# Where the pre-norm weights are applied: in front of the transposes of x on Pool, or behind them on ScalarE and VectorE

## The chip, the cores and the metric

The kernel runs on one core of one Trainium2 chip. The metric is the device time of one execution in microseconds (us), smaller being better. In the profile PE is TensorE (matmuls and transposes), PEld its loading of weights, ACT is ScalarE, DVE is VectorE, POOL is GpSimd and SP is SyncE, which only issues transfers.

## The reference

A model of two layers on x of 256 tokens by 2048 features, all in float32. Around each of the four sub-layers stands an RMS norm on both sides:

```
for layer in range(DEPTH):
    h = rms_norm(x, norm_mix_pre[layer])
    ...
    x = x + rms_norm(m.astype(x.dtype), norm_mix_post[layer])
    h = rms_norm(x, norm_ffn_pre[layer])
    f = swiglu(h, ffn_w_gate[layer], ffn_w_up[layer], ffn_w_down[layer])
    x = x + rms_norm(f.astype(x.dtype), norm_ffn_post[layer])
```

`rms_norm(x, g)` is x / sqrt(mean(x^2) + eps) * g, with g a vector of 2048 weights. The first mixer is a recurrence and an attention side by side, the second an attention with a difference of two maps. What matters here is that h, in each of the four places, is x times the pre-norm weights g, feature by feature, times one number per token. The kernel applies that number (`rstd_x`) when it reads the products, and g before it.

## The kernel before

**Tiles.** Every product is made of slots. A slot is a 512x512 block of a weight matrix (1 MB) against four k tiles of the input, for both halves of the tokens (t = 0 and 1, 128 tokens each). Because float32 is split into a high and a low part, each k tile needs three matmuls, high by high, low weight by high input, high weight by low input: 12 matmuls of 512 columns for one half, 24 for a slot. For a weight, SP loads `raw`, ScalarE writes `w_hi` (function `hi`, L710) and VectorE writes `w_lo` (function `lo`, L1097). A half of a slot is the task `half`, and `half(slot, t, turn)` puts a tile's transposes behind the first three matmuls of the half.

**Boundaries.** Between two sub-layers stands a boundary. There are five: 0 at the start (the chunks of x come from memory), 1 between mixer and FFN of layer 0, 2 between the layers, 3 between mixer and FFN of layer 1, 4 at the end (no input tile is made there). The function `boundary` writes the order of boundaries 1 to 4 out by hand as one list of tasks; every engine walks through the same list and takes its share of each task. s0 to s3 are the last four slots before the boundary (one for each chunk of 512 output features), e, f, g and h the first four slots behind it (one for each chunk of 512 input features), and u is the number of s0. For each chunk c and half t the steps are:

- `add_output`: VectorE adds the product to `yacc` (L1135); `y_square`: ScalarE squares it and sums (L726).
- `rms_y(t)`: VectorE makes the mean (L1113, L1115), Pool the reciprocal root (L1364). It needs the squares of all four chunks of the half.
- `y_gain`: Pool multiplies `yacc` by the post-norm weights (L1372).
- `update(c, t)`: VectorE writes x = x + y * rstd (L1126). Behind it Pool writes x times the pre-norm weights to `tok` (even c) or `stage` (odd c), in `gained` (L1387).
- `turn(c, t)`, a task of kind `T`: PE transposes four blocks of 128x128 from there into one PSUM bank `tp` (L951), ScalarE copies the bank to `h_hi` (L731) and VectorE writes `h_lo`, the bank minus `h_hi` (L1102). I write T00 for c = 0 and t = 0, T10 for c = 1 and t = 0.

The halves behind the boundary come in the order e 0, f 0, e 1, f 1, g 0, g 1, h 0, h 1, and each can start when its tile is ready: T00, T10, T01, T11, T20, T21, T30, T31 (the last half, h 1, needs T31).

The pre-norm weights of a boundary come by a transfer of their own, broadcast to all 128 partitions: 1 MB into `gx` for boundaries 1 to 3 (`gains`), and four pieces of 256 KB at the start, each behind its chunk of x in SP's queue. `gx` holds other things in between, so these transfers wait for Pool's multiplies (`xg_done`).

## Time and profile before

| | us |
|---|---|
| median of 3 runs | 2328.31 (2327.73 to 2328.93) |
| the profiled execution | 2329.11 |
| its span, first to last instruction | 2327.3 |

The span is cut at the instructions; the time of an execution has a little around it. The mean granted clock of TensorE over the span was 0.993, where 1 is 2.4 GHz and 0.5 is 1.2 GHz. A row of a timeline gives the start in us from the span's start, the duration, the engine, the line of the kernel, what it writes and reads, and in square brackets how long the engine was idle before it and who released it. The duration of a matmul includes what overlaps with the next one, so a matmul's share of PE's time is read from start to start.

### The profile page before, as it was taken

The page shows a single profiled execution, that of the slowest core. Times are in us where ns is not written, and L with a number is a line of the kernel's source. Part 1 is how long each engine was busy: PE and PEld are TensorE (multiplying, and loading weights), DVE is VectorE, ACT ScalarE, POOL GpSimd, SP SyncE. Part 2 cuts the span into 40 slices and gives each one's busy share as a digit, 9 for nine tenths or more (in the row PEclk, how much of TensorE's full clock was granted, in tenths as well). Part 3 has the DMA queues.
Part 4 walks back from the last instruction along what each step waited for, and adds up shares of the span by engine and source line. Part 5 has one row for each costly group of instructions (what it writes and reads, how often), then busy time and mean ns, then how long its engine had stood idle before and what let it go on. Part 6 is the DMA issues. An engine that isn't in the chain of part 4 may idle for free.

```text
span 2327.3 us, 27257 instructions
## 1 busy us (share of the span) xinstructions
PE 2273.3 (98%) x10273; PEld 1858.9 (80%) x10273; DVE 1313.6 (56%) x1308; ACT 1033.7 (44%) x1131; POOL 253.3 (11%) x243
## 2 busy tenths in 40 slices
PE   8989999899999999999999999999999999999997
PEld 6877778688888888888777777887888888888886
DVE  4567466654555555554655555676545555555555
ACT  5676444533333333343455555545434333333432
POOL 2463001400000000000340111014000000000002
PEclk9999999999999999999999999999999999999999
DMA  8545344555555555555454444555556555555552
GB/s 277 168 139 168 124 165 153 205 185 188 192 195 184 197 183 197 183 196 191 152 182 153 155 162 144 199 167 187 189 183 196 190 188 193 185 197 182 196 187 102
DMA packets 212263, 417.87 MB, mean 180 GB/s; under 512 B 12040, under 2 KB 12640, under 8 KB 211296
## 3 DMA queue, kind: packets, MB, share of 16 engines
q1 hardware_dynamic: 212192, 416.92, 54.3%
q8 instruction: 45, 0.74, 0.1%
q14 instruction: 26, 0.21, 0.0%
HBM read 414.79 MB, written 2.10 MB: 179 GB/s over the span
## 4 chain that ended last, share of the span: by engine, by line
issue 71%; PE 20%; POOL 4%; DVE 3%; DMA 1%; ACT 1%; SPq 0%; POOLq 0%; DVEq 0%; ACTq 0%
PE acc L937 16%; POOL yacc L1372 1%; PE tp L951 1%; DVE xs L1126 1%; DVE w_lo L1097 1%; PE sc L1018 1%; DMA gq<-in_norm_ffn_post 1%; POOL stage L1387 0%; PE sc L1023 0%; POOL small L1364 0%; PE sc L996 0%; POOL gq L1436 0%; PE pv L996 0%; POOL rot L1406 0%; PE pv L1051 0%
## 5 line engine op out<-in xcount | busy, mean ns | idle before, releaser
L1097 DVE TENSOR_TENSOR w_lo<-raw,w_hi 128x2048 fp32r<-128x2048 f32 x383 | 883.2, 2306 | 512.4 <-PE acc L937 495.3
L710 ACT ACTIVATE w_hi<-raw 128x2048 fp32r<-128x2048 f32 x383 | 734.2, 1917 | 759.5 <-PE acc L937 734.6
L937 PE MATMUL acc<-w_hi,h_hi 128*128 128x512 f32 x2240 | 888.6, 397 | 16.7 <-DVE h_lo L1102 16.7
L937 PE MATMUL acc<-w_hi,h_lo 128*128 128x512 f32 x2240 | 874.7, 390 | 0.0
L937 PE MATMUL acc<-w_lo,h_hi 128*128 128x512 f32 x2240 | 874.4, 390 | 0.0
L937 PEld LDWEIGHTS acc<-w_hi,h_hi 128*128 128x128 f32 x2240 | 422.5, 189 | 111.3 <-DVE h_lo L1102 23.4
L937 PEld LDWEIGHTS acc<-w_hi,h_lo 128*128 128x128 f32 x2240 | 421.7, 188 | 89.1
L937 PEld LDWEIGHTS acc<-w_lo,h_hi 128*128 128x128 f32 x2240 | 422.5, 189 | 84.9 <-issue 0.7
L937 PE MATMUL acc<-w_hi,y_hi 128*128 128x512 f32 x832 | 325.8, 392 | 1.9 <-DVE y_lo L1102 1.9
L937 PE MATMUL acc<-w_hi,y_lo 128*128 128x512 f32 x832 | 323.9, 389 | 0.0
L937 PE MATMUL acc<-w_lo,y_hi 128*128 128x512 f32 x832 | 323.9, 389 | 0.0
L1135 DVE TENSOR_TENSOR yacc<-acc,yacc 128x512 f32<-128x512 f32 x208 | 141.7, 687 | 163.6 <-PE acc L937 163.6
L1372 POOL TENSOR_TENSOR yacc<-yacc,gq 128x512 f32<-128x512 f32 x32 | 48.5, 1522 | 1554.9 <-ACT junk L726 1554.9
L937 PEld LDWEIGHTS acc<-w_hi,y_hi 128*128 128x128 f32 x832 | 156.2, 188 | 37.3 <-issue 2.9
L937 PEld LDWEIGHTS acc<-w_hi,y_lo 128*128 128x128 f32 x832 | 156.2, 188 | 32.6
L937 PEld LDWEIGHTS acc<-w_lo,y_hi 128*128 128x128 f32 x832 | 156.2, 188 | 32.1 <-issue 0.2
L807 ACT ACTIVATE probT<-tp 128x256 f32<-128x256 f32 (+1 forms) x48 | 21.9, 457 | 123.6 <-PE pv L1051 64.4
L900 ACT ACTIVATE y_hi<-tp 128x512 fp32r<-128x512 f32 x44 | 24.2, 596 | 87.8 <-PE tp L951 87.8
L1324 DVE SCALAR_TENSOR_TENSOR tok<-acc,small,stage 128x512 f32<-128x512 f32 x44 | 33.0, 751 | 52.8 <-PE acc L937 52.8
L894 ACT ACTIVATE stage<-acc,small 128x512 f32<-128x512 f32 x44 | 30.2, 690 | 56.6 <-PE acc L937 56.5
L1406 POOL TENSOR_TENSOR rot<-stage,ropes 128x128 f32<-128x128 f32 x24 | 21.7, 902 | 284.3 <-ACT stage L748 283.0
L951 PE MATMUL tp<-ident,tok 128*128 128x128 f32 x288 | 40.1, 278 | 11.7 <-POOL tok L1387 9.4
(142 smaller groups left out, 1058.8 us busy)
## 6 DMA issues: line engine op xcount, KB each, us to landing
raw<-in_ffn_w_gate SPq DMA_DIRECT2D x88, 1024.0 KB, 5.1
raw<-in_ffn_w_up SPq DMA_DIRECT2D x88, 1024.0 KB, 5.1
raw<-in_ffn_w_down SPq DMA_DIRECT2D x88, 1024.0 KB, 5.0
raw<-in_od_w_in SPq DMA_DIRECT2D x48, 1024.0 KB, 5.1
...
```

Of the source, the lines that this page charges most:

```text
L710: act.activation(w_hi[u % HI][:, :, :], raw[u % RAW][:, :, :], ACT.Copy).then_inc(hi_done, 1)
L807: act.activation(flat_pt[:, 0:cols], flat_tp[:, 0:cols], ACT.Copy).then_inc(tp_free[task.e % 2], 1)
L894: act.activation(stage[:, t, :], acc[n % 2][t][:, :], ACT.Silu, scale=rstd_x[:, t:t + 1]).then_inc(acc_free[n % 2][t], 1)
L900: act.activation(y_hi[:, 0:KT, t * P:(t + 1) * P], tp[t][:, :, :], ACT.Copy).then_inc(t_hi, 1)
L937: mm = pe.matmul(acc[n % 2][t][:, :], operand(lhs, a, k, t), w[:, k, :], start=first and k == 0 and j == 0, stop=last and k == KT - 1 and ...
L951: ins = pe.transpose(dst, src, ident[:, :])
L1018: pe.matmul(sc[:, :, :].rearrange("p m t -> p (m t)"), q[:, kt, t * P:(t + 1) * P], keys[task.g % 2][:, kt, :, :].rearrange("p m t -> p (m ...
L1097: dve.tensor_tensor(w_lo[u % LO][:, :, :], raw[u % RAW][:, :, :], w_hi[u % HI][:, :, :].bitcast(F32), ALU.subtract).then_inc(lo_done, 1)
L1126: dve.scalar_tensor_tensor(r, yacc[:, task.t, cols], rstd_y[:, task.t:task.t + 1], r, ALU.mult, ALU.add).then_inc(upd_done, 1)
L1135: dve.tensor_tensor(y, a, y, ALU.add).then_inc(acc_free[n % 2][t], 1)
L1324: dve.scalar_tensor_tensor(tok[:, t, :], acc[n_up % 2][t][:, :], rstd_x[:, t:t + 1], stage[:, t, :], ALU.mult, ALU.mult).then_inc(acc_free ...
L1372: pool.tensor_tensor(y, y, post_gain[:, cols], ALU.mult).then_inc(yg_done, 1)
```

## The change

Pool's multiply in front of the transposes is gone. PE transposes x itself. ScalarE applies the pre-norm weights while it writes the high part: behind the transpose a feature is a partition, so the weights of a 128x128 block are one column, given to ScalarE as a scale. VectorE does the same while it writes the low part. A column fits one block only, so both work in four pieces of 128x128 in place of one of 128x512. The four blocks lie in two PSUM banks, the first two in `tp`, the last two in `sc` or `pv`; VectorE's pieces wait for ScalarE's in pairs (`x_hi`). The weights of all four places come once, at the start, as one transposed array `pre` of 32 KB, prepared with the arrays of constants; the broadcasts to `gx` and the waits on `xg_done` are gone. The hand-written order of a boundary changes in one place: T00 now stands inside the last half before the boundary (s3, t = 1), `add_output` of that half stands behind T00, and `hi(u + 6)` moves behind the last square. `y_gain` waits for the square of its own tile, in place of all the squares listed so far.

```diff
@@ -304,8 +304,8 @@
             tasks += [update(c, 1), update(c + 1, 1), Task("store", c=c, t=1)]
         return tasks
     e, f, g, h = after
-    tasks += [hi(u + 6), update(1, 0), y_square(s2, 1)] + half(s3, 1) + add_output(s3, 1)
-    tasks += [turn(0, 0), y_square(s3, 1), rms_y(1), y_gain(1, 1), lo(u + 5), update(0, 1)]
+    tasks += [update(1, 0), y_square(s2, 1)] + half(s3, 1, turn(0, 0)) + add_output(s3, 1)
+    tasks += [y_square(s3, 1), hi(u + 6), rms_y(1), y_gain(1, 1), lo(u + 5), update(0, 1)]
     tasks += half(e, 0, turn(1, 0)) + [hi(u + 7), update(1, 1)]
     tasks += half(f, 0, turn(0, 1)) + [y_gain(2, 1), square(0, 0), update(2, 0)]
     tasks += half(e, 1, turn(1, 1)) + [y_gain(3, 0), square(1, 0), square(0, 1), lo(u + 6), update(2, 1)]
...
@@ -322,15 +322,17 @@
         if task.kind == "T":
             task.e = plan.e
             plan.e += 1
-            buffer = "tok" if task.src == "tok" or (task.src == "x" and task.g % 2 == 0) else "stage"
-            plan.read[buffer, task.t] = task.e
+            if task.src != "x":
+                plan.read["tok" if task.src == "tok" else "stage", task.t] = task.e
             key = {"x": ("x", task.b), "tok": ("y", task.layer)}.get(task.src, (task.src, task.layer))
             plan.ready[(*key, task.g, task.t)] = task.e
-            if task.src in ("x", "tok"):
+            if task.src == "tok":
                 task.m = plan.m
                 plan.m += 1
             if task.src == "x":
-                task.gained = plan.gained[task.b, task.g, task.t]
+                task.m = plan.xm
+                task.update = plan.update.get((task.b, task.g, task.t))
+                plan.xm += KT
         elif task.kind == "pt":
             task.e = plan.e
             plan.e += 1
...
@@ -343,8 +345,10 @@
             task.sq, task.update = plan.squares, plan.update.get((task.b, task.c, task.t))
             task.stat = plan.stat.get(("rms_x", task.b - 1, 0))
             plan.squares += 1
+            if task.kind == "y_square":
+                plan.squared[task.b, task.slot.cb, task.t] = plan.squares
         elif task.kind == "y_gain":
-            task.sq, task.gained = plan.squares, plan.y_gains
+            task.sq = plan.squared[task.b, task.c, task.t]
             plan.y_gained[task.b, task.c, task.t] = plan.y_gains
             plan.y_gains += 1
         if task.kind in ("evac", "silu"):
...
@@ -580,8 +584,10 @@
                 return [b[:, kt:kt + KT, t * P:(t + 1) * P] for b in (h_hi, h_lo)]
             return [b[:, KT * task.g:KT * (task.g + 1), t * P:(t + 1) * P] for b in (y_hi, y_lo)]
 
-        def x_buffer(c):
-            return tok if c % 2 == 0 else stage
+        def input_tile(e, k):
+
+            bank = tp[e % 2] if k < KT // 2 else (sc, pv)[e % 2][:, :, :].rearrange("p a (b c) -> p (a b) c", b=2)
+            return bank[:, k, :]
 
 
         @block.sync
...
@@ -601,7 +607,6 @@
 
                 cols = slice(c * KC, (c + 1) * KC)
                 sp.dma_start(xs[:, :, cols], x_rows[:, :, cols]).then_inc(x_in[c], 16)
-                sp.dma_start(pre_gain[:, cols], norm_mix_pre[0, cols].partition_broadcast(P)).then_inc(x_in[c], 16)
 
             def load_parameters():
...
@@ -631,14 +636,8 @@
                     sp.wait_ge(rg_out, RG_OUT * AT)
                 else:
                     sp.wait_ge(yg_done, 8 * (b - 1))
-                    sp.wait_ge(xg_done, 8 * b)
-                if b == 3:
-                    sp.wait_ge(s_done, 16 + 3 * HEADS_OF_GROUP)
                 post = norm_mix_post[b // 2] if b % 2 else norm_ffn_post[b // 2 - 1]
-                sp.dma_start(post_gain, post.partition_broadcast(P)).then_inc(gain_in[0], 16)
-                if b < 4:
-                    pre = norm_ffn_pre[b // 2] if b % 2 else norm_mix_pre[b // 2]
-                    sp.dma_start(pre_gain, pre.partition_broadcast(P)).then_inc(gain_in[1], 16)
+                sp.dma_start(post_gain, post.partition_broadcast(P)).then_inc(gain_in, 16)
 
             def load_slot(slot):
                 block = NF - 1 if slot.w == "down" else slot.kg
...
@@ -747,8 +747,21 @@
                     func = ACT.Gelu_apprx_tanh if task.what == "gate" else ACT.Copy
                     act.activation(dst, acc[slot][t][:, :], func, scale=rstd_x[:, t:t + 1]).then_inc(acc_free[slot][t], 1)
 
+            def input_hi(task):
+
+                act.wait_ge(pre_in, 16)
+                act.wait_ge(tp_done, task.e + 1)
+                dst = region_of(task)[0]
+                for k in range(KT):
+                    kt = KT * task.g + k
+                    act.activation(dst[:, k, :], input_tile(task.e, k), ACT.Copy,
+                                   scale=pre[:, task.b, kt:kt + 1]).then_inc(x_hi, 1)
+
             def transposed(task):
-                if task.src in ("x", "tok"):
+                if task.src == "x":
+                    input_hi(task)
+                    return
+                if task.src == "tok":
                     operand_hi(task)
                     return
                 act.wait_ge(tp_done, task.e + 1)
...
@@ -964,8 +975,11 @@
                     product(slot.u, slot.n, slot.lhs, slot.first, slot.last, task.t, task.k)
                 elif task.kind == "T":
                     if task.src == "x":
-                        pe.wait_ge(xg_done, task.gained + 1)
-                        src = x_buffer(task.g)
+                        if task.b:
+                            pe.wait_ge(upd_done, task.update + 1)
+                        else:
+                            pe.wait_ge(x_in[task.g], 16)
+                        src = xs[:, :, task.g * KC:(task.g + 1) * KC]
                     elif task.src == "tok":
                         if task.layer == 0:
                             pe.wait_ge(o_done, task.head + 1)
...
@@ -978,7 +992,10 @@
                             pe.wait_ge(rope_done, task.evac.rope + task.t + 1)
                         else:
                             wait_acc(pe, task.evac.n, task.t)
-                    transposes(task.e, quarter(task.e, src, task.t))
+                    if task.src == "x":
+                        transposes(task.e, [(input_tile(task.e, k), src[:, task.t, k * P:(k + 1) * P]) for k in range(KT)])
+                    else:
+                        transposes(task.e, quarter(task.e, src, task.t))
                 elif task.kind == "par" and task.i == 0:
 
                     pe.wait_ge(par_in, 16 * 12)
...
@@ -1101,6 +1118,16 @@
                 dve.wait_ge(t_hi, m + 1 + NT * it)
                 dve.tensor_tensor(lo_ap, tp[e % 2][:, :, :], hi_ap.bitcast(F32), ALU.subtract).then_inc(tp_free[e % 2], 1)
 
+            def input_lo(task):
+
+                hi_ap, lo_ap = region_of(task)
+                for k in range(KT):
+                    kt = KT * task.g + k
+                    dve.wait_ge(x_hi, task.m + k // 2 * 2 + 2)
+                    ins = dve.scalar_tensor_tensor(lo_ap[:, k, :], input_tile(task.e, k), pre[:, task.b, kt:kt + 1],
+                                                   hi_ap[:, k, :].bitcast(F32), ALU.mult, ALU.subtract)
+                ins.then_inc(tp_free[task.e % 2], 1)
+
             def mean(task):
 
                 if task.kind == "rms_x":
...
@@ -1366,25 +1395,10 @@
             def y_gain(task):
 
                 pool.wait_ge(sq_done, task.sq)
-                pool.wait_ge(gain_in[0], 16 * task.b)
+                pool.wait_ge(gain_in, 16 * task.b)
                 cols = slice(task.c * KC, (task.c + 1) * KC)
                 y = yacc[:, task.t, cols]
                 pool.tensor_tensor(y, y, post_gain[:, cols], ALU.mult).then_inc(yg_done, 1)
-
-            def gained(task):
-
-                if task.b == 4:
-                    return
-                if task.b == 0:
-                    pool.wait_ge(x_in[task.c], 32)
-                else:
-                    pool.wait_ge(upd_done, task.update + 1)
-                    pool.wait_ge(gain_in[1], 16 * task.b)
-                last = (task.stage_free if task.c % 2 else task.tok_free)[task.t]
-                if last is not None:
-                    pool.wait_ge(tp_done, last + 1)
-                cols = slice(task.c * KC, (task.c + 1) * KC)
-                pool.tensor_tensor(x_buffer(task.c)[:, task.t, :], xs[:, task.t, cols], pre_gain[:, cols], ALU.mult).then_inc(xg_done, 1)
 
             def rotate(task):
...
@@ -1439,15 +1453,12 @@
 
             def zero_keys():
 
-                pool.wait_ge(xg_done, 8 * 3)
                 pool.wait_ge(s_done, 16)
                 for buf in keys:
                     pool.memset(buf[:, :, :, :], 0.0).then_inc(keys_zero, 1)
 
             def task_of(task):
-                if task.kind == "update":
-                    gained(task)
-                elif task.kind == "y_gain":
+                if task.kind == "y_gain":
                     y_gain(task)
                 elif task.kind in ("rms_x", "rms_y"):
                     rsqrt(task)
...
@@ -1460,15 +1471,11 @@
                 elif task.kind == "heads":
                     pool.wait_ge(sub_var_done, task.g + 1)
                     pool.tensor_tensor(sub_r, sub_var, minus_half, ALU.pow).then_inc(sub_rstd, 1)
-                if task.kind == "update" and task.b == 0 and task.c == NC - 1 and task.t == NT - 1:
-
-
-                    for i in range(2):
-                        pool.memset(rg_w[i], 0.0).then_inc(zero_done, 1)
-                    pool.wait_ge(xg_done, 8)
-                    pool.memset(xrT[:, :, 0:CONV // 2], 0.0).then_inc(zero_done, 1)
-                    pool.memset(xrT[:, :, CONV // 2 + T:XP], 0.0).then_inc(zero_done, 1)
-
+
+            for i in range(2):
+                pool.memset(rg_w[i], 0.0).then_inc(zero_done, 1)
+            pool.memset(xrT[:, :, 0:CONV // 2], 0.0).then_inc(zero_done, 1)
+            pool.memset(xrT[:, :, CONV // 2 + T:XP], 0.0).then_inc(zero_done, 1)
             for part in plan.parts:
                 for task in part.tasks or ():
                     task_of(task)
...
@@ -1504,6 +1511,8 @@
     arrays["log_count"] = log_counts()
     arrays["rope"] = rope_tables()
     arrays["identity"] = np.eye(P, dtype=np.float32)
+    pre = np.stack([arrays["norm_mix_pre"], arrays["norm_ffn_pre"]], axis=1)
+    arrays["pre_T"] = np.ascontiguousarray(pre.reshape(4, D // P, P).transpose(2, 0, 1))
     args = [nc.dram_tensor(f"in_{n}", a.shape, mybir.dt.from_np(a.dtype), kind="ExternalInput").ap()
             for n, a in arrays.items()]
     args.append(nc.dram_tensor("out_0", arrays["x"].shape, F32, kind="ExternalOutput").ap())
```

The places in the order of instructions, first on PE, at the end of slot s3 in boundary 1 (acc11 is the sum of s3 for t = 1, acc00 that of e for t = 0). Before:

```order
L937 MATMUL acc11<-w_hi3,h_hi 128x512
L937 MATMUL acc11<-w_lo1,h_hi 128x512
L937 MATMUL acc11<-w_hi3,h_lo 128x512
L951 MATMUL tp0<-ident,tok 128x128 x4
L937 MATMUL acc00<-w_hi0,h_hi 128x512
L937 MATMUL acc00<-w_lo2,h_hi 128x512
L937 MATMUL acc00<-w_hi0,h_lo 128x512
```

Now:

```order
L948 MATMUL acc01<-w_hi2,h_lo 128x512
L948 MATMUL acc11<-w_hi3,h_hi 128x512
L948 MATMUL acc11<-w_lo1,h_hi 128x512
L948 MATMUL acc11<-w_hi3,h_lo 128x512
L962 MATMUL tp0<-ident,xs 128x128 x2
L962 MATMUL sc<-ident,xs 128x128 x2
L948 MATMUL acc11<-w_hi3,h_hi 128x512
L948 MATMUL acc11<-w_lo1,h_hi 128x512
L948 MATMUL acc11<-w_hi3,h_lo 128x512
L948 MATMUL acc11<-w_hi3,h_hi 128x512
L948 MATMUL acc11<-w_lo1,h_hi 128x512
```

T00 has moved ahead of nine matmuls of the last half; its four transposes read x, and write two banks.

On VectorE, at the same place, from the first update of the boundary on. Before:

```order
L1126 SCALAR_TENSOR_TENSOR xs<-yacc,small,xs 128x512
L1135 TENSOR_TENSOR yacc<-acc,yacc 128x512
L1126 SCALAR_TENSOR_TENSOR xs<-yacc,small,xs 128x512
L1135 TENSOR_TENSOR yacc<-acc,yacc 128x512
L1102 TENSOR_TENSOR h_lo<-tp,h_hi 128x4x128
L1113 TENSOR_REDUCE small<-small 128x1
L1115 TENSOR_SCALAR small<-small 128x1
L1097 TENSOR_TENSOR w_lo<-raw,w_hi 128x2048
L1126 SCALAR_TENSOR_TENSOR xs<-yacc,small,xs 128x512
L1102 TENSOR_TENSOR h_lo<-tp,h_hi 128x4x128
L1126 SCALAR_TENSOR_TENSOR xs<-yacc,small,xs 128x512
```

Now (the lines have moved: L1153 is the update, L1162 `add_output`, L1127 the pieces of a tile, L1114 a weight's low part):

```order
L1153 SCALAR_TENSOR_TENSOR xs<-yacc,small,xs 128x512
L1162 TENSOR_TENSOR yacc<-acc,yacc 128x512
L1153 SCALAR_TENSOR_TENSOR xs<-yacc,small,xs 128x512
L1127 SCALAR_TENSOR_TENSOR h_lo<-tp,pre,h_hi 128x128 x2
L1127 SCALAR_TENSOR_TENSOR h_lo<-sc,pre,h_hi 128x128 x2
L1162 TENSOR_TENSOR yacc<-acc,yacc 128x512
L1140 TENSOR_REDUCE small<-small 128x1
L1142 TENSOR_SCALAR small<-small 128x1
L1114 TENSOR_TENSOR w_lo<-raw,w_hi 128x2048
L1153 SCALAR_TENSOR_TENSOR xs<-yacc,small,xs 128x512
L1127 SCALAR_TENSOR_TENSOR h_lo<-tp,pre,h_hi 128x128 x2
```

The add in front of the mean (L1113 before, L1140 now) has gone from ahead of T00 to behind it.

On ScalarE, from the last squares of the boundary's first half of tokens on. Before:

```order
L726 ACTIVATE junk,small<-yacc 128x512 x2
L710 ACTIVATE w_hi<-raw 128x2048
L726 ACTIVATE junk,small<-yacc 128x512
L731 ACTIVATE h_hi<-tp 128x4x128
L726 ACTIVATE junk,small<-yacc 128x512
L731 ACTIVATE h_hi<-tp 128x4x128
L710 ACTIVATE w_hi<-raw 128x2048
L731 ACTIVATE h_hi<-tp 128x4x128
```

Now:

```order
L710 ACTIVATE w_hi<-raw 128x2048
L726 ACTIVATE junk,small<-yacc 128x512 x3
L757 ACTIVATE h_hi<-tp,pre 128x128 x2
L757 ACTIVATE h_hi<-sc,pre 128x128 x2
L726 ACTIVATE junk,small<-yacc 128x512
L710 ACTIVATE w_hi<-raw 128x2048
L757 ACTIVATE h_hi<-tp,pre 128x128 x2
L757 ACTIVATE h_hi<-pv,pre 128x128 x2
```

The weight's high part (L710) that stood ahead of the last square but one stands behind the last one, and a tile is four instructions.

## Rows read from the trace of the kernel before

**Rows 1.** The page: each engine's busy time, its share of the span, its instructions

```profile
PE 2273.3 (98%) x10273; PEld 1858.9 (80%) x10273; DVE 1313.6 (56%) x1308; ACT 1033.7 (44%) x1131; POOL 253.3 (11%) x243
```

**Rows 2.** List of waits: us in total, times, longest

```profile
PE acc L937 <- DVE h_lo L1102: 16.7, 16, 2.0
```

**Rows 3.** Timeline of PE, boundary 1: start us, us, what, idle before it

```profile
406.45 0.39 PE L937 MATMUL acc<-w_hi,h_hi 128*128 128x512 f32 x1
...
408.94 0.39 PE L937 MATMUL acc<-w_hi,h_lo 128*128 128x512 f32 x1
409.62 0.66 PE L951 MATMUL tp<-ident,tok 128*128 128x128 f32 x4 [0.29 <-POOL tok L1387]
411.69 0.50 PE L937 MATMUL acc<-w_hi,h_hi 128*128 128x512 f32 x1 [1.41 <-DVE h_lo L1102]
...
414.79 0.40 PE L937 MATMUL acc<-w_hi,h_lo 128*128 128x512 f32 x1
416.98 0.50 PE L937 MATMUL acc<-w_hi,h_hi 128*128 128x512 f32 x1 [1.79 <-DVE h_lo L1102]
...
427.50 0.50 PE L937 MATMUL acc<-w_hi,h_hi 128*128 128x512 f32 x1 [0.65 <-DVE h_lo L1102]
...
432.72 0.50 PE L937 MATMUL acc<-w_hi,h_hi 128*128 128x512 f32 x1 [1.72 <-DVE h_lo L1102]
...
436.61 0.50 PE L937 MATMUL acc<-w_hi,h_hi 128*128 128x512 f32 x1 [0.40 <-DVE h_lo L1102]
```

**Rows 4.** Timeline of DVE, boundary 1

```profile
407.44 0.75 DVE L1126 SCALAR_TENSOR_TENSOR xs<-yacc,small,xs 128x512 f32<-128x512 f32 x1 [0.69 <-POOL small L1364]
...
410.04 0.68 DVE L1135 TENSOR_TENSOR yacc<-acc,yacc 128x512 f32<-128x512 f32 x1
410.94 0.69 DVE L1102 TENSOR_TENSOR h_lo<-tp,h_hi 128x512 fp32r<-128x512 f32 x1 [0.23 <-ACT h_hi L731]
...
411.83 2.29 DVE L1097 TENSOR_TENSOR w_lo<-raw,w_hi 128x2048 fp32r<-128x2048 f32 x1
414.57 1.76 DVE L1126 SCALAR_TENSOR_TENSOR xs<-yacc,small,xs 128x512 f32<-128x512 f32 x1 [0.44 <-POOL small L1364]
416.25 0.68 DVE L1102 TENSOR_TENSOR h_lo<-tp,h_hi 128x512 fp32r<-128x512 f32 x1
...
428.69 3.38 DVE L1097 TENSOR_TENSOR w_lo<-raw,w_hi 128x2048 fp32r<-128x2048 f32 x1
```

**Rows 5.** Timeline of ACT, boundary 1

```profile
408.88 0.63 ACT L726 ACTIVATE junk<-yacc 128x512 bf16<-128x512 f32 x1
...
410.31 0.60 ACT L731 ACTIVATE h_hi<-tp 128x512 fp32r<-128x512 f32 x1 [0.70 <-PE tp L951]
```

**Rows 6.** Timeline of POOL, boundary 1

```profile
429.88 3.33 POOL L1387 TENSOR_TENSOR stage<-xs,gx 128x512 f32<-128x512 f32 x1
```

**Rows 7.** Timeline of DVE, attention of layer 1, pieces of 128x128

```profile
1302.32 2.19 DVE L1198 SCALAR_TENSOR_TENSOR tok<-tok,small,sub_gain 128x128 f32<-128x128 f32 x8 [1.76 <-POOL small L1462]
```

**Rows 8.** Timeline of ACT, attention of layer 1, sizes without a scale column

```profile
1249.61 0.39 ACT L807 ACTIVATE probT<-tp 128x256 f32<-128x256 f32 x1 [3.52 <-PE pv L1051]
1249.89 0.30 ACT L817 ACTIVATE probT<-tok 128x128 f32<-128x128 f32 x1
```

**Rows 9.** Timeline of ACT, recurrence, with a column as operand

```profile
159.23 0.47 ACT L842 ACTIVATE yacc<-sc,par 128x256 f32<-128x256 f32 x1 [0.17 <-PE pv L996]
```

**Rows 10.** Timeline of PE, boundary 2

```profile
1158.55 0.50 PE L937 MATMUL acc<-w_hi,h_hi 128*128 128x512 f32 x1 [0.23 <-DVE h_lo L1102]
```

**Rows 11.** Timeline of PE, recurrence of layer 0

```profile
155.41 2.08 PE L996 MATMUL sc<-gq 128*128 128x256 f32 x4 [5.51 <-POOL gq L1436]
```

**Rows 12.** Busy time by window; behind POOL stands the granted clock (PEclk)

```profile
153.50:160.30 6.80, 4.89 (x12) 3.89 (x13) 3.23 (x4) 3.74 (x7) 6.33 (x7) 0.50 0.00 0
1153.60:1157.00 3.40, 3.40 (x12) 2.73 (x11) 2.96 (x2) 1.51 (x2) 3.40 (x2) 0.50 0.10 7
```

**Rows 13.** Timeline of all engines, start of the kernel

```profile
11.64 0.80 PE L937 MATMUL acc<-w_hi,h_hi 128*128 128x512 f32 x1 [2.02 <-DVE h_lo L1102]
```

25 lines of the change are left out of this document (13 added, 12 removed).

## The prediction

> **What bounds the kernel now.** I read the page first. TensorE is busy for 98% of the span, so what can be won or lost is its idle time; DVE, at 56%, is far from full on average [rows 1]. The list of waits then says where TensorE idles for this part of the program: `PE acc L937 <- DVE h_lo L1102`, 16 waits, 16.7 us in all [rows 2]. That is a matmul waiting for the low part of an input tile, which is what the change rebuilds. Third I read the timeline of PE across the boundary at 405 to 441 us (mixer to FFN of layer 0) [rows 3]. Matmuls start every 0.227 us (12 from 406.45 to 408.94), except for five pauses, each released by `h_lo`: before the half of slot e at 411.69 (1.41 us), of f at 416.98 (1.79), of g at 427.50 (0.65) and 432.72 (1.72), of h at 436.61 (0.40). Together 6.0 us. I call them e0, f0, g0, g1, h0. Boundaries 2 and 3 have the same five, with a shorter one ahead of f0 (0.23 us in boundary 2, [rows 10]); why is said below.
>
> Last I read the timeline of DVE there [rows 4], to see why `h_lo` is late. DVE is busy back to back: an update of x, a weight's low part (L1097), a tile's low part (L1102). Two things stretch it. The update that runs beside nothing takes 0.75 us, the one at 414.57 beside Pool's multiply takes 1.76; and L1097 takes 2.29 us alone (411.83) but 3.38 beside Pool (428.69; Pool's own multiply runs from 429.88 for 3.33 us) [rows 4, 6]. So the boundary is a chain on DVE, not on Pool: Pool's multiply ahead of T00 costs PE only a pause of 0.29 us at 409.62 [rows 3].
>
> **Pool's part.** 8 multiplies fall away at each boundary. I take an update beside which they ran at 0.75 us and L1097 at 2.29, except where one of the four multiplies by the post-norm weight (L1372) still runs: these now follow each other directly behind the second rsqrt, so the update at 414.57 keeps its 1.76 us.
>
> **A tile's part.** Today ScalarE starts the high part at 410.31 and the low part ends at 410.94 + 0.69 = 411.63: 1.32 us for a tile, 0.68 of it DVE's [rows 4, 5]. After it there are four pieces of 128x128 on each engine. DVE has a row of that operation and size: eight in 2.19 us, 0.35 each and 0.26 from start to start [rows 7], so four take 0.35 + 3 x 0.26 = 1.13 us, 0.45 more than the whole tile. ScalarE has no such row. 128x128 without a scale column took 0.30 us; 128x256 took 0.39 without and 0.47 with a column, so the column costs 0.08; starts lie 0.11 closer than durations [rows 8, 9]. That gives 0.38 us, 0.27 from start to start. DVE's first piece may begin when two are done, at 0.27 + 0.38 = 0.65; its third when four are, at 1.19. With 0.03 us to be released the low part ends at 1.22 + 0.26 + 0.35 = 1.83 us behind ScalarE's start, 0.5 later than today.
>
> The Trainium skill, "ScalarE: Activation LUTs", section "What ACT_TABLE_LOAD costs", prices an ACTIVATE with one pointer operand at about 280 ns + 0.833 ns per element, with neighbours overlapping by 93 ns. By that a piece would be an estimated 0.39 us, 0.29 from start to start, and a tile would end 0.1 us later than in my sum; the nearest rows here agree to 0.01 us in the duration. By the page the total would be about 0.5 us higher.
>
> **The moved tile.** T00 now stands behind the first three matmuls of the last half before the boundary, on PE. Those end at 406.45 + 0.68 = 407.13, but the first update ends at 408.19 (407.44 + 0.75), so T00 starts at 408.27 and PE pauses 1.14 us inside that half. A half without a tile takes 2.72 us (406.45 to 408.94, + 0.23), one with a tile 3.33 (411.69 to 414.79, + 0.23), so a tile takes 0.61. The half ends at 408.27 + 0.61 + 9 x 0.227 = 410.92, in place of 409.17 [rows 3, 4]. ScalarE takes T00 only behind the square that it starts at 408.88 [rows 5], so at 409.51; the low part ends at 411.34 and e0 starts at 411.40: 0.29 us won.
>
> What is late next is the second half of tokens. `add_output` of that half, before at 410.04 and in front of T00's low part, now stands behind it on DVE: 411.26 to 411.94. The square, the mean and then L1097 follow it; today L1097 starts 1.11 us behind the end of the add (411.83 against 410.72) [rows 4], so now 413.05, 1.22 later. Behind it on DVE are queued the update at 414.57, now 415.79, and the low part of tile T10, which started at 416.25, now 417.47, and takes 1.13: 418.60. f0 waits for it: 418.66 against 416.98, **1.68 us lost**. `hi(u+6)` on ScalarE, moved behind the last square, ends by 415, and its low part is wanted at 425: nothing.
>
> From there, in the same way:
> - from f0 on come two halves without a pause today; a tile's way within a half (0.7 us of matmuls, 0.1, 0.69 from transpose to ScalarE, 1.83) is 3.3 us, just the length of a half. No loss, and no slack either.
> - g0 stands behind a weight (2.29), an update (0.75) and T20 (1.13), starts overlapping by 0.08, from 425.03 on: 429.14 against 427.50, 1.64 late.
> - g1: behind an update, a weight and a tile, 3.93 us in place of today's 5.22 (427.50 to 432.72): 433.07, 0.35 late. Here the relief from Pool pays, 1.3 us.
> - h0: 3.93 in place of 3.89: 0.39 late. h1 is bound by PE.
>
> So each boundary ends 0.4 us later at full clock, 1.2 us for three.
>
> **The clock.** PE's pause ahead of f0 grows from 1.96 (414.79 + 0.23 to 416.98) to 3.93 us (414.73 to 418.66). In boundary 2 the granted clock stands at 0.50, 1.2 GHz, from 1153.60 to 1157.00, behind the pause ahead of e0 [rows 12]; its cost is swallowed there, f0 still waits 0.23 us for `h_lo` at 1158.55 [rows 10]. Boundary 1 has the same pause at full clock. A longer pause, 5.51 us up to 155.41 [rows 11], has the clock at 0.50 from 153.50 to 160.30, so for 4.9 us of the work behind it [rows 12]. For 3.9 us I take the lower clock as likely, and as reaching 1.0 to 3.4 us into f0: at half rate this costs 0.5 to 1.7 us, and nothing swallows it, because f0 and the two halves behind it are bound by PE. I take 1.2: 3.6 us for three.
>
> **The start and the queues.** The first matmul, at 11.64, waits for `h_lo`, which is made behind the first weights [rows 13]. Of 1344 KB queued up to those weights (512 for x, 256 for `gx`, 64 for the identity, 512 of weights) 256 leave and 32 come, a sixth of less than 8 us; the first tile ends up to 0.45 us later on DVE. I take 0.3 us won, between 0 and 0.9. Three transfers of 1 MB (`gx`) also leave SP's queue, and their waits with them; none of the five pauses was ended by a transfer, so nothing. The looser wait of `y_gain` changes nothing where Pool stands behind the second rsqrt anyway. The last boundary has no tiles: nothing.
>
> **Sum**: 1.2 + 3.6 - 0.3 = 4.5 us. The profiled execution took 2329.11 us (span 2327.3), so 2333.6 in its terms; it stands 0.80 above the median of the runs, 2328.31, so 2332.8.
>
> **Bounds.** A piece on DVE lies between 0.17 us (a quarter of today's 0.68) and 0.75 (a whole update, alone); I stay with the row of its own shape. On ScalarE between 0.15 (a quarter of 0.60) and 0.47. With the lower ends a tile costs as today: four tiles on DVE's chain, 0.45 each, 1.8 us a boundary, and the clock may hold: 2323. With ScalarE's upper end and 1.7 us for the clock: about 1.5 us more a boundary, 2337; a DVE piece of 0.40 adds another 2.
>
> **The rivals.**
> - *Forecast*, 35%: 2332.8.
> - *The clock holds ahead of f0*, 25%: 1.2 - 0.3 alone, 2329.2. For it speaks boundary 1, which kept 2.4 GHz through a pause like that of the other two.
> - *Small pieces are dear, or the lower clock costs its full 1.7 us*, 28%: 2337 to 2339. For it speaks that tiles have no slack inside a half, so each 0.1 us more is paid at about six tiles of a boundary.
> - *Relief from Pool decides, faster*, 12%: 2322.3. Place: g0, g1 and h0, where weights fall from 3.38 to 2.29 us on DVE. If a tile stays at about 0.68 us there and the clock holds, f0 is 1.22 late, DVE is through with T20 before PE needs it, so g0 at 428.05, g1 at 431.38 and h0 at 434.71 are bound by PE alone, the last 1.9 us ahead of today: 5.7 for three, 0.3 at the start. It decides below about 0.75 us for a tile on DVE. Against it is the row of eight pieces at 0.26 us from start to start.
>
> Anything within 0.2% (4.7 us) can't be told from no change. Above 2333.0 lie the case of dear pieces and about half of the forecast's own spread: slower 0.45, same 0.43, faster 0.12. Range 2325 to 2339; it leaves out most of the faster case.
>
> **What would show it.** In the changed kernel's profile: four pieces near 0.38 us on ScalarE and 0.35 on DVE per tile; T00 on PE right behind an update, with a pause of about 1.1 us inside a half; f0 10.5 us behind the end of the boundary's first update (408.19 to 418.66) where it was 8.8; a granted clock of 0.5 just behind f0's pause; weights at 2.29 us throughout g and h. I am wrong if f0 isn't later than today relative to that update, which would mean that DVE's order there isn't what holds the second half, or if a tile on DVE costs well off 1.13 us.

## The result and the profile after

The changed kernel takes 2337.59 us (median of 6 runs, 2334.85 to 2338.42) against 2328.1 (6 runs, 2327.73 to 2328.93): 0.4% slower, ratio 1.0037 (95% interval 1.0027 to 1.0047). The profiled execution took 2336.99 us, 7.9 more than that of before. The medians differ by 9.5: the profiled execution of before stands 1.0 above its median and the changed kernel's 0.6 below, so 1.6 us of the loss are in neither of the two traces. The page and the list of waits (us in total, times, longest), as [rows 1, 2]:

```profile
span 2335.2 us, 27407 instructions
PE 2277.3 (98%) x10273; PEld 1860.3 (80%) x10273; DVE 1311.3 (56%) x1404; ACT 1049.5 (45%) x1227; POOL 198.6 (9%) x211
...
PE acc L948 <- DVE h_lo L1127: 21.5, 18, 3.8
```

Pool lost 55 us of work and DVE a little, and neither shows in the time. PE waits 4.8 us more for the low parts of the input tiles. The timeline of PE at boundary 1 (start, duration, what, idle before it), as [rows 3]:

```profile
408.01 0.39 PE L948 MATMUL acc<-w_hi,h_lo 128*128 128x512 f32 x1
409.34 0.44 PE L962 MATMUL tp<-ident,xs 128*128 128x128 f32 x2 [0.95 <-DVE xs L1153]
...
412.43 0.50 PE L948 MATMUL acc<-w_hi,h_hi 128*128 128x512 f32 x1 [0.38 <-DVE h_lo L1127]
...
415.52 0.40 PE L948 MATMUL acc<-w_hi,h_lo 128*128 128x512 f32 x1
419.67 0.50 PE L948 MATMUL acc<-w_hi,h_hi 128*128 128x512 f32 x1 [3.75 <-DVE h_lo L1127]
...
421.17 0.63 PE L948 MATMUL acc<-w_lo,h_hi 128*128 128x512 f32 x1
421.60 0.63 PE L948 MATMUL acc<-w_hi,h_lo 128*128 128x512 f32 x1
```

Three things are to be seen. T00 makes PE pause inside the half (409.34 - 408.01 - 0.227 = 1.1 us). The pause ahead of f0 has grown to 419.67 - 415.52 - 0.23 = 3.92 us. And 1.5 us into f0 the matmuls start every 0.43 us instead of every 0.227. What f0 waits for stands on DVE, as [rows 4]:

```profile
408.54 0.75 DVE L1153 SCALAR_TENSOR_TENSOR xs<-yacc,small,xs 128x512 f32<-128x512 f32 x1 [0.68 <-POOL small L1393]
...
411.25 0.61 DVE L1127 SCALAR_TENSOR_TENSOR h_lo<-tp,pre,h_hi 128x128 fp32r<-128x128 f32 x2 [0.70 <-ACT h_hi L757]
411.78 0.60 DVE L1127 SCALAR_TENSOR_TENSOR h_lo<-sc,pre,h_hi 128x128 fp32r<-128x128 f32 x2
412.29 0.68 DVE L1162 TENSOR_TENSOR yacc<-acc,yacc 128x512 f32<-128x512 f32 x1
413.83 0.16 DVE L1140 TENSOR_REDUCE small<-small 128x1 f32<-128x4 f32 x1 [0.85 <-ACT junk L726]
414.02 0.15 DVE L1142 TENSOR_SCALAR small<-small 128x1 f32<-128x1 f32 x1
414.10 2.29 DVE L1114 TENSOR_TENSOR w_lo<-raw,w_hi 128x2048 fp32r<-128x2048 f32 x1
416.83 1.75 DVE L1153 SCALAR_TENSOR_TENSOR xs<-yacc,small,xs 128x512 f32<-128x512 f32 x1 [0.44 <-POOL small L1393]
418.50 0.59 DVE L1127 SCALAR_TENSOR_TENSOR h_lo<-tp,pre,h_hi 128x128 fp32r<-128x128 f32 x2
419.02 0.59 DVE L1127 SCALAR_TENSOR_TENSOR h_lo<-pv,pre,h_hi 128x128 fp32r<-128x128 f32 x2
```

The `add_output` at 412.29 stands behind T00's low part, and everything behind it is queued: mean, weight, update, T10. It starts 3.00 us behind the end of the boundary's first update (409.29), where it stood 1.85 behind it before (410.04 against 408.19): 1.15 us later. T10's four pieces, from 418.50 to 419.61, then take 0.4 us more than the one operation did. Together that is the 1.6 us that f0 comes later. ScalarE's pieces of T00 and Pool's two operations beside this stretch, as [rows 5, 6]:

```profile
410.61 0.61 ACT L757 ACTIVATE h_hi<-tp,pre 128x128 fp32r<-128x128 f32 x2
411.11 0.62 ACT L757 ACTIVATE h_hi<-sc,pre 128x128 fp32r<-128x128 f32 x2
```

```profile
414.25 2.54 POOL L1393 TENSOR_TENSOR small<-small 128x1 f32<-128x1 f32 x1 [5.75 <-DVE small L1142]
416.77 4.64 POOL L1401 TENSOR_TENSOR yacc<-yacc,gq 128x512 f32<-128x512 f32 x3
```

Busy time by window, the granted clock (PEclk) behind POOL, in the stretches behind f0's pause of boundaries 1, 2 and 3, as [rows 12]:

```profile
421.10:424.50 3.40, 3.40 (x9) 2.64 (x8) 1.79 (x5) 1.75 (x6) 1.56 (x2) 0.50 0.00 0
...
1161.80:1168.60 6.80, 5.43 (x15) 4.36 (x16) 3.76 (x11) 1.87 (x7) 4.35 (x3) 0.50 0.37 139
...
1588.40:1591.80 3.40, 3.04 (x9) 2.56 (x10) 0.96 (x3) 0.44 (x2) 3.33 (x3) 0.51 0.48 187
```

At each boundary of this execution TensorE runs at 1.2 GHz behind that pause.

In the table below all starts are of PE, in us from the end of the boundary's first update (boundary 1; 408.19 before, 409.29 after), with the kernels of the experiments, which the next section describes. A column is a half (e1 is slot e, t = 1; f1 is left out), a row is a kernel (e1 is an experiment). The last column is the time from the last matmul of e0's half to f0, less the 0.23 us of that matmul; in w1 it is filled with transposes.

| | e0 | f0 | e1 | g0 | g1 | h0 | h1 | pause ahead of f0 |
|---|---|---|---|---|---|---|---|---|
| before | 3.50 | 8.80 | 12.10 | 19.32 | 24.53 | 28.42 | 31.75 | 1.96 |
| after | 3.15 | 10.38 | 15.26 | 22.38 | 26.28 | 30.18 | 33.52 | 3.92 |
| w1 | 3.15 | 10.39 | 13.74 | 20.98 | 24.88 | 28.78 | 32.12 | 3.94 |
| e1 | 3.52 | 9.32 | 12.67 | 19.91 | 23.81 | 27.71 | 31.07 | 0.95 |
| e3 | 3.08 | 8.37 | 11.70 | 18.10 | 21.41 | 24.95 | 28.26 | 1.98 |
| b1 | 5.55 | 12.70 | 18.67 | 25.09 | 30.07 | 33.96 | 37.29 | 3.95 |
| c1 | 3.14 | 8.19 | 12.07 | 19.31 | 23.20 | 27.10 | 30.44 | 1.74 |
| v1 | 3.61 | 8.51 | 11.74 | 18.43 | 21.87 | 25.21 | 28.55 | 0 |
| v4 | 3.61 | 7.54 | 10.88 | 17.57 | 21.02 | 24.35 | 27.69 | 0.61 |

### The profile page after: what moved, and what is told of

The parts are those of the page before. It is cut to its first block, busy times and chain, and to the rows that moved or that the text cites. A ratio compares the mean times of both kernels' runs of the same rounds, so it can differ in the third digit from the quotient of the medians.

```text
span 2335.2 us, 27407 instructions
## 1 busy us (share of the span) xinstructions
PE 2277.3 (98%) x10273; PEld 1860.3 (80%) x10273; DVE 1311.3 (56%) x1404; ACT 1049.5 (45%) x1227; POOL 198.6 (9%) x211
## 4 chain that ended last, share of the span: by engine, by line
PE 58%; issue 33%; DVE 4%; POOL 2%; ACT 2%; DMA 1%; SPq 0%; DVEq 0%; ACTq 0%; POOLq 0%
PE acc L948 53%; PE tp L962 2%; DVE w_lo L1114 2%; PE sc L1035 1%; PE sc L1040 1%; DVE h_lo L1127 1%; DVE xs L1153 1%; PE pv L1063 1%; PE pv L1068 0%; POOL small L1393 0%; PE sc L1013 0%; POOL gq L1450 0%; PE pv L1013 0%; ACT w_hi L710 0%; POOL rot L1420 0%
## 5 line engine op out<-in xcount | busy, mean ns | idle before, releaser
L1114 DVE TENSOR_TENSOR w_lo<-raw,w_hi 128x2048 fp32r<-128x2048 f32 x383 | 876.5, 2289 | 508.7 <-PE acc L948 494.1
L710 ACT ACTIVATE w_hi<-raw 128x2048 fp32r<-128x2048 f32 x383 | 734.3, 1917 | 752.3 <-PE acc L948 737.6
L1162 DVE TENSOR_TENSOR yacc<-acc,yacc 128x512 f32<-128x512 f32 x208 | 141.6, 687 | 163.7 <-PE acc L948 163.7
L905 ACT ACTIVATE stage<-acc,small 128x512 f32<-128x512 f32 x44 | 30.2, 690 | 56.6 <-PE acc L948 56.4
L806 ACT ACTIVATE prob<-sc,small 128x256 f32<-128x256 f32 x64 | 29.8, 471 | 26.1 <-DVE small L1180 26.1
```

What stands on the lines that cost most here:

```text
L710: act.activation(w_hi[u % HI][:, :, :], raw[u % RAW][:, :, :], ACT.Copy).then_inc(hi_done, 1)
L806: ins = act.activation(prob[:, m, :], sc[:, m, :], ACT.Exp, scale=SCALE, bias=nmx[:, m:m + 1], accum_out=den[n % 2][:, m:m + 1])
L905: act.activation(stage[:, t, :], acc[n % 2][t][:, :], ACT.Silu, scale=rstd_x[:, t:t + 1]).then_inc(acc_free[n % 2][t], 1)
L1114: dve.tensor_tensor(w_lo[u % LO][:, :, :], raw[u % RAW][:, :, :], w_hi[u % HI][:, :, :].bitcast(F32), ALU.subtract).then_inc(lo_done, 1)
L1162: dve.tensor_tensor(y, a, y, ALU.add).then_inc(acc_free[n % 2][t], 1)
```

## The experiments

The change has two halves: the new order, and the weights in pieces in place of Pool's multiply. Four kernels take them apart. Times are medians; kernel before, beside them, 2328.47.

**e1: the old order in the changed kernel.**

```diff
-    tasks += [update(1, 0), y_square(s2, 1)] + half(s3, 1, turn(0, 0)) + add_output(s3, 1)
-    tasks += [y_square(s3, 1), hi(u + 6), rms_y(1), y_gain(1, 1), lo(u + 5), update(0, 1)]
+    tasks += [hi(u + 6), update(1, 0), y_square(s2, 1)] + half(s3, 1) + add_output(s3, 1)
+    tasks += [turn(0, 0), y_square(s3, 1), rms_y(1), y_gain(1, 1), lo(u + 5), update(0, 1)]
```

> The changed kernel with the order of the boundary as it was: T00 behind the last half, the add of that half and hi(u+6) in front of it. Theory A (the moved tile holds up the second half of tokens on DVE, and the longer pause ahead of f0 lowers the clock): f0 comes 9.4 us behind the end of the boundary's first update (changed kernel 10.4, kernel before 8.8), the pause ahead of it falls from 4 to about 2.5 us, and the time is 1.0 us a boundary less at full clock plus what the clock gives back: 2329 to 2335, most likely 2332. Theory B (the dear pieces are the cause, the order costs nothing): 2337, with f0 at 10.4 us.

Measured 2328.56 us, ratio 1.0002 (0.9993 to 1.0011): no different from before, and better than I expected. PE's pauses at boundary 1 ahead of f0, g0 and g1:

```profile
417.61 0.50 PE L948 MATMUL acc<-w_hi,h_hi 128*128 128x512 f32 x1 [0.76 <-DVE h_lo L1127]
428.20 0.50 PE L948 MATMUL acc<-w_hi,h_hi 128*128 128x512 f32 x1 [0.43 <-DVE h_lo L1127]
432.10 0.50 PE L948 MATMUL acc<-w_hi,h_hi 128*128 128x512 f32 x1 [0.41 <-DVE h_lo L1127]
```

All of the loss is the order's, 9.0 us. With it away, f0 is 0.5 us late by T00's and T10's pieces, and the relief from Pool ahead of g1 more than pays that back: each of the three boundaries ends 0.5 to 0.6 us earlier than before. The pieces at the start of the kernel take that away again (see below).

**e2 and e3: the pre-norm weights left out** (x is transposed into one bank and split as it is, one operation per tile and engine). They don't compute the model; they price the pieces. e2 has the new order, e3 the old.

```diff
...
-                for k in range(KT):
...
-                    act.activation(dst[:, k, :], input_tile(task.e, k), ACT.Copy,
-                                   scale=pre[:, task.b, kt:kt + 1]).then_inc(x_hi, 1)
+                act.activation(dst, tp[task.e % 2][:, :, :], ACT.Copy).then_inc(x_hi, KT)
...
+                dve.tensor_tensor(lo_ap, tp[task.e % 2][:, :, :], hi_ap.bitcast(F32), ALU.subtract).then_inc(tp_free[task.e % 2], 1)
```

> The changed kernel in its new order, but each input tile is one copy and one subtraction of 128x512 again, from one bank, so the pre-norm weights are left out of the computation. Theory A: the pieces cost 0.45 us a tile on DVE; without them the start gains about 1.5 us, f0 is 9.5 us behind the first update and still behind a long pause, g and h are bound by PE: 2325 to 2330. If the order were the only cause, 2336.

> As the run with whole tiles, but with the order of the boundary as it was (the pre-norm weights are left out). Theory A: f0 about 8.5 us behind the first update, no pause long enough to lower the clock for work that isn't hidden, Pool's relief of 1.3 us a boundary or more is won in full: 2320 to 2324. If Pool's multiply had cost DVE nothing, it would be no faster than 2327.

e2 took 2326.92 us (0.9994, 0.9985 to 1.0003), with f0 at 9.8. In its boundary 1 PE's pause was nearly as long as the changed kernel's, and yet the clock held behind it; in boundaries 2 and 3, with pauses of the same length, it fell to 0.5. Boundary 1:

```profile
416.92 0.50 PE L944 MATMUL acc<-w_hi,h_hi 128*128 128x512 f32 x1 [3.58 <-DVE h_lo L1121]
...
416.90:420.00 3.10, 3.08 (x15) 2.57 (x16) 1.97 (x3) 1.21 (x3) 3.10 (x3) 1.00 0.57 218
```

e3 took 2316.94 us (0.995, 0.9937 to 0.9964). e3 was faster than expected: from f0 to g1 PE has no pause left, as my rival of a relief from Pool had it, and no boundary shows the lower clock. Its only two pauses of over 0.3 us at boundary 1:

```profile
411.09 0.50 PE L944 MATMUL acc<-w_hi,h_hi 128*128 128x512 f32 x1 [1.49 <-DVE h_lo L1121]
416.38 0.50 PE L944 MATMUL acc<-w_hi,h_hi 128*128 128x512 f32 x1 [1.83 <-DVE h_lo L1121]
```

So the pieces cost 11.6 us in the old order (2328.56 - 2316.94) and 10.7 in the new (2337.59 - 2326.92), and the order costs 10.0 us with whole tiles too. Apart from the transfers of the weights and `y_gain`'s looser wait, e3 is the kernel before without Pool's multiply, so that multiply costs some 11.5 us (2328.47 - 2316.94): what the change takes away at Pool and what it adds in pieces are equal within the noise, and the order is what is left.

**b1: the new order in the kernel before**, the reverse of e1's edit.

> The kernel before, Pool's multiply included, with only the order of the boundary changed as in the change. Theory A: the last half ends 3.1 us later (412.3 for 409.2), so its add, square and mean and with them f0 come about 2.3 us later, and the pause ahead of f0 grows to 3.7 us and lowers the clock: about 4 us a boundary, 2340. Theory B, the order is innocent: 2328.

Measured 2343.75 us, 1.0058 (1.0045 to 1.0072). f0 is 3.9 us later than before in boundaries 1 and 2 and 2.3 in boundary 3; I had 2.3 for all. e0 is 2.0 us later as well, in 1 and 2, and 0.5 in 3. The granted clock in boundary 1 is 0.5 for 3.4 us from 409.3, behind a pause of 2.3 us inside the last half (T00 waits for Pool), and again for 6.8 us from 419.6; in boundary 3 it held inside the last half. The order alone costs 15.3 us where Pool multiplies ahead of the transposes, so it isn't a gain that the pieces hide.

**w1: PE kept busy in f0's pause.** 32 transposes of the identity, into a bank that nothing reads, behind e0. DVE's chain is untouched. Kernel before, beside w1 and v1 to v3: 2328.35.

```diff
+WARM = 32
...
-    tasks += half(e, 0, turn(1, 0)) + [hi(u + 7), update(1, 1)]
+    tasks += half(e, 0, turn(1, 0)) + [Task("warm"), hi(u + 7), update(1, 1)]
...
+                elif task.kind == "warm":
+                    for k in range(WARM):
+                        pe.transpose(sc[:, 0, 0:P], ident[:, :], ident[:, :])
```

> The changed kernel with 32 extra transposes of the identity (about 3.5 us at the full clock) in PE's pause of 3.9 us ahead of f0, at the three boundaries; they feed nothing. If the lower clock behind that pause costs what the profiles say (1.6, 2.5 and 1.4 us), f0 stays 10.4 us behind the first update, the granted clock stays at 1.0 behind it, and 4 to 5.5 us come back: 2332 to 2334. Rival: the clock falls for other reasons, or the extra transposes delay f0: 2337 or above.

Measured 2332.15 us, 1.0016 (1.0007 to 1.0025), as expected. Windows of w1 at boundary 1, of which the first covers the pause:

```profile
412.00:420.00 8.00, 7.72 (x52) 6.70 (x53) 6.45 (x10) 5.36 (x8) 6.26 (x4) 1.00 0.36 119
420.00:424.00 4.00, 4.00 (x23) 3.17 (x21) 1.79 (x5) 1.76 (x6) 2.18 (x2) 1.00 0.07 28
```

f0 starts at the same place, e1 follows it by 3.35 us instead of 4.88, and the clock stays at 2.4 GHz. What is left per boundary is 0.5 us in each of the three. So the lower clock cost 5.4 us of the 9.5 (2337.59 - 2332.15).

**c1: one update behind T10 instead of ahead of it**, nothing else. Kernel before, beside c1 and v4: 2328.26.

```diff
-    tasks += [y_square(s3, 1), hi(u + 6), rms_y(1), y_gain(1, 1), lo(u + 5), update(0, 1)]
-    tasks += half(e, 0, turn(1, 0)) + [hi(u + 7), update(1, 1)]
+    tasks += [y_square(s3, 1), hi(u + 6), rms_y(1), y_gain(1, 1), lo(u + 5)]
+    tasks += half(e, 0, turn(1, 0)) + [hi(u + 7), update(0, 1), update(1, 1)]
```

> The changed kernel with one task moved in each of boundaries 1 to 3: update(0, 1) stands behind the half of slot e (and so behind tile T10 on VectorE) in place of ahead of it. The chain on VectorE that f0 waits for in the changed kernel is add, weight (2.29 us), mean, update (1.75 us beside Pool), four pieces of T10 (1.13). Theory (that chain, one item at a time, sets f0): f0 falls by the 1.7 us of the update, from 10.38 to about 8.7 us behind the end of the boundary's first update, PE's pause ahead of it from 3.9 to about 2.2 us; T01 has the length of a half to wait for the update, so e1 keeps its place behind f0. At least 3 x 1.7 = 5 us less only if nothing later takes it back: in the changed kernel g0, g1, h0 and h1 are bound by the same chain from T11 on, so that part of it comes back as waits ahead of g0. With the clock: a pause of 2.2 us may or may not bring the half rate. Most likely 2331, between 2328 and 2335. Rival (f0 waits for T10's transposes or for ScalarE): f0 stays at 10.4 and the time at 2337.5.

Measured 2328.05 us, 0.9998 (0.9989 to 1.0007): 9.5 us below the changed kernel, at the lower end of what I gave. DVE at boundary 1:

```profile
415.74 2.29 DVE L1114 TENSOR_TENSOR w_lo<-raw,w_hi 128x2048 fp32r<-128x2048 f32 x1
417.94 0.60 DVE L1127 SCALAR_TENSOR_TENSOR h_lo<-tp,pre,h_hi 128x128 fp32r<-128x128 f32 x2
418.46 0.60 DVE L1127 SCALAR_TENSOR_TENSOR h_lo<-pv,pre,h_hi 128x128 fp32r<-128x128 f32 x2
418.98 2.93 DVE L1153 SCALAR_TENSOR_TENSOR xs<-yacc,small,xs 128x512 f32<-128x512 f32 x2
```

T10 now starts where the weight ends. It wins not only the update (1.75 us) but also DVE's wait for Pool's reciprocal root ahead of it (0.44), so f0 is 2.19 us earlier and its pause, 1.7 us, kept the full clock in all three boundaries. The chain of f0 is shown by this: one item taken out of it moved f0 by that item and the wait ahead of it. The rival, that ScalarE or the transposes hold f0, falls, and with it the thought that `hi(u + 6)`, which now stands ahead of T10 on ScalarE, holds f0. Against w1, where the clock held too, c1 is 4.1 us shorter: so much of the 9.5 us is the chain itself, and 5.4 are the clock.

**v1: the updates and Pool's multiplies in an order of their own.** `pool_wait` makes Pool wait for an update before its next multiply, so that the two don't run beside each other.

```diff
-    tasks += [update(1, 0), y_square(s2, 1)] + half(s3, 1, turn(0, 0)) + add_output(s3, 1)
-    tasks += [y_square(s3, 1), hi(u + 6), rms_y(1), y_gain(1, 1), lo(u + 5), update(0, 1)]
-    tasks += half(e, 0, turn(1, 0)) + [hi(u + 7), update(1, 1)]
-    tasks += half(f, 0, turn(0, 1)) + [y_gain(2, 1), square(0, 0), update(2, 0)]
+    tasks += [pool_wait(0, 0), y_gain(1, 1), y_gain(3, 0), hi(u + 6), update(1, 0), y_square(s2, 1)]
+    tasks += half(s3, 1) + add_output(s3, 1)
+    tasks += [y_gain(2, 1), turn(0, 0), y_square(s3, 1), rms_y(1), lo(u + 5)]
+    tasks += half(e, 0, turn(1, 0)) + [hi(u + 7), update(0, 1), update(1, 1)]
+    tasks += half(f, 0, turn(0, 1)) + [pool_wait(1, 1), y_gain(3, 1), square(0, 0), update(2, 0), update(2, 1), update(3, 0)]
...
```

> The changed kernel with a new order of the boundary, everything computed: T00 behind the last half again, the update (0,1) behind tile T10, three updates ahead of tile T11, weights' low parts behind the tile that is wanted next, Pool's four multiplies drawn forward. If f0 waits for the chain of rsqrt, update and tile on DVE and not for DVE's whole work, f0 comes 7.0 us behind the first update without a pause, h1 27 us (31.1 with the old order), 4 us less a boundary: 2316. Rival: the boundary is bound by the sum of DVE's work, whatever its order: 2326 to 2328.

Measured 2320.92 us, 0.9968 (0.9956 to 0.998), faster than both kernels, but 5 us short of what I expected. PE's only pause of over 0.2 us at boundary 1, the window behind it, and what runs on DVE and Pool there:

```profile
413.08 0.50 PE L952 MATMUL acc<-w_hi,h_hi 128*128 128x512 f32 x1 [2.02 <-DVE h_lo L1131]
...
414.20:417.60 3.40, 3.40 (x11) 2.73 (x10) 3.40 (x7) 2.88 (x5) 2.12 (x1) 0.50 0.13 17
...
413.22 2.69 DVE L1118 TENSOR_TENSOR w_lo<-raw,w_hi 128x2048 fp32r<-128x2048 f32 x1
...
409.56 4.21 POOL L1405 TENSOR_TENSOR yacc<-yacc,gq 128x512 f32<-128x512 f32 x3 [0.86 <-DVE xs L1157]
```

The multiplies drawn forward stretch the weight at 413.22 to 2.69 us (2.29 alone), and e0's pause brings 1.2 GHz in boundaries 1 and 3: f0 is at 8.51 there and at 7.52 in boundary 2, where the clock held. I had 7.0 for all three; the rest of what is missing was not taken apart.

**v2: v1 with a later low part and later squares at the start**, to take away two of PE's waits there.

> As the run before, and at the start of the kernel the squares of x come later on ScalarE and the fourth weight's low part behind tile T30 on DVE. The start had won 1.5 us at the second half and lost 1.9 in two pauses of 0.9 us ahead of the third and fourth slot; if these come from DVE's queue they go: 1.5 us below the run before, 2314.5. Rival: 2316, no change.

Measured 2320.67 us, 0.9968 (0.9956 to 0.998), the same as v1: the rival was right, the pauses only moved to another slot.

**v3: v1's order in the kernel before**, Pool's multiply kept.

> The kernel before, with Pool's multiply and whole tiles, in the same new order of the boundary. It tells what the change is worth once the order is right. If Pool's multiplies beside DVE still stretch the weights' low parts from 2.3 to 3.3 us and put Pool's 1.3 us between an update and its tile, 2318 to 2322, above the changed kernel in that order. Rival: tiles of one piece are worth more than Pool's relief: below 2316.

Measured 2328.5 us, 1.0001 (0.9992 to 1.001): far off what I expected. Pool's timeline, and the transposes that wait for it:

```profile
409.98 3.31 POOL L1391 TENSOR_TENSOR stage<-xs,gx 128x512 f32<-128x512 f32 x1
...
413.35 1.11 PE L955 MATMUL tp<-ident,stage 128*128 128x128 f32 x4 [3.16 <-POOL stage L1391]
```

The multiply for T10 runs beside DVE's weight for 3.31 us, PE waits for it inside e0's half, and f0 comes at 11.8, where v1 has 8.5. Behind that wait the granted clock is 0.5 for 6.8 us in all three boundaries:

```profile
410.00:416.80 6.80, 3.64 (x11) 2.90 (x11) 3.85 (x4) 2.31 (x2) 5.27 (x5) 0.51 0.44 154
```

Here the change of the weights itself is worth something: 7.6 us, 2328.5 against 2320.92. How much of that is the clock was not separated.

**v4: v1 with 16 transposes of the identity in e0's pause**, against 2328.26 before.

```diff
-    tasks += [y_gain(2, 1), turn(0, 0), y_square(s3, 1), rms_y(1), lo(u + 5)]
+    tasks += [y_gain(2, 1), turn(0, 0), y_square(s3, 1), rms_y(1), lo(u + 5), Task("warm")]
```

> The version with moved updates, and 16 transposes of the identity into a bank that nothing reads, on PE in the pause ahead of e0 of boundaries 1 to 3. It computes everything. Theory (the half rate that boundaries 1 and 3 showed behind e0's pause of 2 us costs 1 us each, because f0 has no pause left that swallows it): no granted clock of 0.5 in the boundaries, e0 as before or up to 0.1 us later, about 2 us less: 2319, between 2318 and 2321. Rival (the half rate behind e0 is swallowed by f0's wait): 2321 or slightly above, as without the transposes.

Measured 2318.6 us, 0.996 (0.9946 to 0.9974), the fastest that computes everything: 9.7 us below before, 19.0 below the changed kernel. Windows of v4 at boundary 1:

```profile
409.00:413.00 4.00, 3.72 (x27) 3.13 (x27) 3.97 (x10) 2.48 (x8) 4.00 (x4) 1.00 0.02 6
413.00:417.00 4.00, 3.55 (x19) 2.64 (x18) 4.00 (x7) 2.95 (x5) 2.37 (x1) 1.00 0.17 31
```

No boundary shows the lower clock; f0 is at 7.54 in all three, 0.97 earlier than v1's 8.51, in the two boundaries where v1 lost it.

## Why the prediction was right, and where its sizes were off

The time forecast was 2332.8 and came out at 2337.6: slower, as I gave the largest chance (0.45, with 0.43 for no change), 4.8 us above the sum and inside the range. The mechanism was right and its size was not: the loss is 9.5 us by the medians, twice the 4.5 of the sum, and 7.9 in the profiled executions. That the time still fell inside the range is in part luck: its upper end, 2339, stood for dearer single pieces, which didn't come. By its steps:

- **The moved tile: right.** PE's pause for T00 was to be 1.14 us, it is 1.10. e0 was to start 3.21 us behind the update's end, it starts at 3.15. The add was to start 3.07 behind it; it starts at 412.29 - 409.29 = 3.00.
- **f0: right.** 10.47 forecast, 10.38 measured, pause 3.93 against 3.92. c1 shows the mechanism.
- **A tile's part: right.** ScalarE 0.36 us a piece and 0.25 from start to start (0.38 and 0.27 forecast); DVE 0.35 and 0.26 as in the row I took; T00 from ScalarE's start to the low part's end 412.38 - 410.61 = 1.77 us (1.83). The Trainium skill, "ScalarE: Activation LUTs", section "What ACT_TABLE_LOAD costs", made that an estimated 0.39 and 0.29; the trace lies below it, and the rows of this kernel were the better price.
- **Relief from Pool, g0 to h1: right in the net.** g1 and h0 follow at 3.90 us (3.93 forecast), weights beside them take 2.28. At full clock a boundary ends 0.5 us later (w1), 0.4 forecast. But that is a difference of two sizes that were both too small: by the starts of h1 in the table, Pool's relief alone is 3.5 us a boundary (31.75 before, 28.26 in e3), where my rival had 1.9, and the pieces alone cost 2.8 (31.07 in e1), where my bounds had 1.8. That they cancel was luck.
- **The clock: right in kind, too small.** The term was 3.6 us for three; w1 against the changed kernel gives 5.4. I let 1.0 to 3.4 us of the work behind f0's start run at half rate. It was 3.4 us in boundary 1 (421.10 to 424.50), 5.4 in boundary 2 (f0 starts at 1163.17, the stretch ends at 1168.60) and 3.0 in boundary 3 (1588.76 to 1591.80). Against w1, e1 starts 1.5, 2.5 and 1.4 us later behind f0, and the boundaries end 1.4, 2.4 and 1.3 us later.
- **The start: wrong sign.** The term was 0.3 us won. The first matmul is 1.10 us earlier than before, and yet the ninth half starts 0.39 us later. Where the first weight lands varies by 2 us between profiled executions of all kernels, with no order by change; so I read from the first high part on ScalarE to the ninth half's start. That takes 30.2 to 31.0 us in the five kernels with whole tiles and 32.3 to 33.5 in the seven with pieces. The pieces cost some 2 us at the start that the sum didn't have. In the changed kernel's trace most of them are two pauses of PE, which the trace before doesn't have:

```profile
26.83 0.50 PE L948 MATMUL acc<-w_hi,h_hi 128*128 128x512 f32 x1 [0.69 <-DVE h_lo L1127]
34.26 0.50 PE L948 MATMUL acc<-w_hi,h_hi 128*128 128x512 f32 x1 [0.76 <-DVE h_lo L1127]
```

There, two tiles follow each other on DVE behind a weight, 2.2 us in place of 1.3. I had costed the pieces in boundaries 1 to 3 and, at the start, for the first tile only, though boundary 0 has eight tiles too.

- **What is left.** Between the ninth half and boundary 1 the profile after lost another 0.7 us, in the recurrence, which the change doesn't touch. The same stretch gained 1.1 us in w1 and lost 0.0 in v4, so I take it for scatter; that was not tested. The sum of the parts, 0.4 at the start, 0.7, and 1.9, 2.9 and 1.8 for the boundaries, is 7.7, and the spans differ by 7.9.

Of the rivals, the third (2337 to 2339) gave the time that was measured. It had two legs. Dear pieces didn't come: a piece took 0.36 and 0.35 us, and at full clock a boundary ended where the forecast said. The other leg, the lower clock at its full 1.7 us a boundary or 5.1 for three, did: w1 has 5.4. The start, which no rival had, made up some 2 us more. A clock that holds gave 2329.2; w1 forced that and took 2332.15; some 2 of the 2.9 us between are the pieces at the start, and what the rest is stays open. The relief from Pool was real, 11.5 us, but was eaten by the pieces, 11.6: with the weights left out (e3) it decides, to 2316.9.
